# Narrow projections in feature rows with transposes, and unused matmuls at five borders, in a two-block forward pass

## What is computed

```python
# first block
x   = macaron_ffn(x, mod[:, 0:3], *ffn1)          # norm, gate/up (2816), down
ctx = macaron_ffn(ctx, mod_ctx[:, 0:3], *ffn1)
h_ctx_f, h_ctx_b = context_states(ctx, ...)       # h @ w_in[:, x | B | dt]: dt has 2*12 = 24 columns
x, _, _ = mix_sublayer(x, mod[:, 3:6], h_ctx_f, h_ctx_b, *mix)
x = macaron_ffn(x, mod[:, 6:9], *ffn2)
# mix_sublayer: u_f, z, xbc, dt_raw = split(h @ w_in); conv, scan over chunks, fourier part, @ w_out
dt = softplus(dt_raw + dt_bias)                   # (512, 24)
# second block, two layers
h = rmsnorm(x, attn_norm[l]); z = h @ w_in[l]     # q/k/v of four branches A B C D, gates
# vB (64 columns), wI (4, weights of the index heads) and fA (8, forget logits) are narrow; vD has 128
score = einsum('bqhs,bqh->bqs', relu(qI . kI), wI * scale); sel = top_k(score, 128)   # branch B
logf  = log_sigmoid(fA + forget_bias)             # branch A
x = x + sum_n(sigmoid(gate_n) * (y_n @ w_branch_n)) @ w_out[l]
h = rmsnorm(x, ffn_norm[l]); x = x + (silu(a) * b) @ w_down[l]   # a, b from a causal conv of h @ w_up
```

## Time and profile before

| quantity | value |
|---|---|
| median of 3 runs | 3680.62 us (3677.23 to 3682.32) |
| the profiled execution's own time | 3679.27 us |
| its span (first to last instruction) | 3677.9 us |
| mean granted clock of PE | 0.972 of full speed |
| busy: PE, PEld, DVE, ACT, POOL | 3492.6, 2784.7, 1684.8, 1434.5, 1426.5 us |

### The profile page before, as it was taken

The page is one execution under the profiler, slowest core; times in us unless marked ns, Lnnn a source line. Parts: engine busy times, 40 slices in busy tenths (PEclk is TensorE's granted clock), DMA queues, the critical chain, the costliest instruction groups (busy, mean ns, idle before and its releaser), DMA issues.

```text
span 3677.9 us, 45245 instructions
## 1 busy us (share of the span) xinstructions
PE 3492.6 (95%) x17424; PEld 2784.7 (76%) x17424; DVE 1684.8 (46%) x2997; ACT 1434.5 (39%) x2448; POOL 1426.5 (39%) x651
## 2 busy tenths in 40 slices
PE   6899999998899998999999999999999999999998
PEld 4788889786578886876776778887876766778886
DVE  7976464547420115846453243133755453234143
ACT  3223354554532323344443344343344453334342
POOL 3454434321244444334332344444333333344443
PEclk9999999999999998999999999999999999999999
DMA  7574345131123322222222222323222222223232
GB/s 301 193 255 145 124 156 176 64 96 54 46 80 92 103 92 82 87 68 83 75 74 86 88 81 91 100 90 111 83 73 75 73 76 93 80 75 101 95 96 82
DMA packets 118423, 376.45 MB, mean 102 GB/s; under 512 B 15424, under 2 KB 16320, under 8 KB 117952
## 3 DMA queue, kind: packets, MB, share of 16 engines
q1 hardware_dynamic: 107280, 356.33, 29.4%
q10 hardware_dynamic: 10928, 17.22, 1.6%
HBM read 359.86 MB, written 2.10 MB: 98 GB/s over the span
## 4 chain that ended last, share of the span: by engine, by line
PE 76%; DVE 11%; ACT 5%; issue 3%; POOL 2%; DMA 2%; ACTq 1%; SPq 0%; DVEq 0%; POOLq 0%
PE ps L1336 23%; PE ps L1338 22%; PE ps L1337 22%; DVE b L2197 2%; ACT b L1663 2%; POOL b L2561 1%; PE ps L1579 1%; PE ps L1600 1%; ACTq L1769 1%; PE ps L1561 1%; DVE b L2463 1%; PE ps L1623 1%; PE ps L1557 1%; PE ps L1634 1%; DMA b<-in_w 1%
## 5 line engine op out<-in xcount | busy, mean ns | idle before, releaser
L2561 POOL TENSOR_TENSOR b<-b,b 128x1024 fp32r<-128x1024 f32 (+2 forms) x579 | 1326.1, 2290 | 2141.2 <-ACT b L1663 2124.3
L1336 PE MATMUL ps<-b,b 128*128 128x512 f32 (+3 forms) x4848 | 1839.6, 379 | 76.9 <-POOL b L2561 27.5
L1338 PE MATMUL ps<-b,b 128*128 128x512 f32 (+3 forms) x4848 | 1800.4, 371 | 0.0
L1337 PE MATMUL ps<-b,b 128*128 128x512 f32 (+3 forms) x4848 | 1800.3, 371 | 0.0
L1336 PEld LDWEIGHTS ps<-b,b 128*128 128x128 f32 x4848 | 932.0, 192 | 312.3 <-issue 113.3
L1338 PEld LDWEIGHTS ps<-b,b 128*128 128x128 f32 x4848 | 931.3, 192 | 159.5
L1337 PEld LDWEIGHTS ps<-b,b 128*128 128x128 f32 x4848 | 932.6, 192 | 154.6 <-issue 5.0
L1663 ACT ACTIVATE b<-b 128x1024 fp32r<-128x1024 f32 (+2 forms) x622 | 607.2, 978 | 388.9 <-PE ps L1338 254.5
L2112 DVE SCALAR_TENSOR_TENSOR b<-ps,b,b 128x511 f32<-128x511 f32 x88 | 66.0, 750 | 366.7 <-ACT b L1714 366.7
L2197 DVE CUSTOM_DVE_ANT_0 b<-b,b,b 128x1024 bf16<-128x1024 f32 x112 | 216.8, 1936 | 18.0 <-DMA b<-in_ada 6.2
L1724 ACT ACTIVATE b<-b 128x512 fp32r<-128x512 f32 (+1 forms) x110 | 64.9, 590 | 397.2 <-DVE b L2121 294.5
(11 more groups left out here) (231 smaller groups left out, 2371.9 us busy)
## 6 DMA issues: line engine op xcount, KB each, us to landing
b<-in_w SPq DMA_DIRECT2D x458, 512.0 KB, 3.5
b<-in_ada SPq DMA_DIRECT2D x88, 512.0 KB, 5.0
b<-in_w SPq DMA_DIRECT2D x80, 384.0 KB, 3.1
b<-in_w SPq DMA_DIRECT2D x80, 320.0 KB, 2.9
b<-b ACTq DMA_DIRECT2D x176, 64.0 KB, 2.0
b<-in_const SPq DMA_DIRECT2D x24, 256.0 KB, 4.0
b<-in_x SPq DMA_DIRECT2D x1, 2048.0 KB, 16.6
out<-b SPq DMA_DIRECT2D x8, 256.0 KB, 2.5
```

The lines of the kernel that those rows point to most:

```text
L1336: pe.matmul(out, a[0], b[0], start=first, stop=False)
L1337: pe.matmul(out, a[0], b[1], start=False, stop=False)
L1338: return pe.matmul(out, a[1], b[0], start=False, stop=last)
L2561: then(pool.tensor_tensor(wlo[j % NS][:, 0:nk * w], raw[j % NR][:, 0:nk * w], whi[j % NS][:, 0:nk * w].bitcast(F32), ALU.subtract), "lop", j)
```

## The change

The narrow projections `dt`, `cdt`, `vb` and `vd` are now made by `fm` with M = 24, 76 or 128 stationary columns and all tokens streaming (24 matmuls each in place of 96, or of 48 for `cdt`). ACT copies the M x tokens tile out of PSUM (event `nt`), and a step `back`, put behind the next tile's matmuls, transposes it on PE in blocks of 128 tokens (4 or 2 transposes) and copies it to where its readers expect it: on DVE with the bias for `dt` and `cdt`, on ACT for `vb` and `vd`. The readers `wi` and `fg1` come later in the list (behind six gaps, in the thread of `qa`), `fg2` behind the first eight steps of the selection, and the context's softplus (`sp`, s="c") behind `row` and a gap. At the five borders `idle` steps issue matmuls on the high half of the next weight piece, whose results nobody reads: 8 ahead of a `nfin` whose squares DVE adds up, 12 behind each `nfin`, and 3 behind each square of norms 7 and 9. That makes 56 at the first and at the second border and 20 at each other one, 172 in all.

```diff
+    def narrow(self, name, key, ver, N, M, **kw):
+        t = self.fm(name, 0, key, ver, N, M=M, **kw)
+        self.settle()
+        self.step("evac", t=t)
+        self.late.append(dict(kind="back", t=t))
...
+def prenorm(p, c=None):
     nid = PN[p]["norm"]
-    return [do("nfin", nid=nid)] + [do("pn", p=p, i=i) for i in range(8)] + [do("pnlow", p=p)]
+    return (idle(c, 0 if nid in PLAIN else 8) + [do("nfin", nid=nid)] + idle(c, 12)
+            + [do("pn", p=p, i=i) for i in range(8)] + [do("pnlow", p=p)])
+
+def addnorm(a, c=None):
+    return (idle(c, 8) + [do("nfin", nid=AN[a]["norm"])] + idle(c, 12) + [do("an", a=a, i=i) for i in range(8)])
+
+def squares(nid, c=None):
+    return [x for i in range(8) for x in [do("nadd", nid=nid, i=i)] + idle(c, 3)]
...
-    F.tm("dt", 1, "dt", ("pn", 2), 4)
+    F.narrow("dt", "dt", ("pn", 2), L, 24)
+    late, F.late = F.late, []
     S += weave(F)
     F = fore()
+    F.late = late
...
-    F.tm("cdt", 1, "cdt", ("pn", 3), 2)
+    F.narrow("cdt", "cdt", ("pn", 3), LC, 24)
...
-    S += weave(F, [do("sp", s="c"), do("row")] + [do("grp", g=g) for g in range(4)]
+    S += weave(F, [do("row"), do("gap"), do("sp", s="c")] + [do("grp", g=g) for g in range(4)]
...
-    S += weave(F) + addnorm(2) + squares(7) + prenorm(4)
-    S += weave(ffn(2, "ffn2", ("pn", 4), L, 8)) + addnorm(3) + squares(9) + prenorm(5)
+    c = at[0]
+    S += weave(F) + addnorm(2, c) + squares(7, c) + prenorm(4, c)
+    F = ffn(2, "ffn2", ("pn", 4), L, 8)
+    c = at[0]
+    S += weave(F) + addnorm(3, c) + squares(9, c) + prenorm(5, c)
...
-        F.tm("vb", 1, "vbwf", H, 4, l=l)
-        S += weave(F) + [do("wi", l=l)]
+        F.narrow("vb", "vbwf", H, L, 76, l=l)
...
-        F.tm("vd", 1, "vd", H, 4, l=l)
-        S += weave(F, [do("fg1", l=l)] + [do("gap")] * 8 + [do("fg2", l=l)] + select(1) + select(2) + select(3), 1.0)
+        F.narrow("vd", "vd", H, L, 128, l=l)
+        late, F.late = F.late, []
+        B = select(1) + select(2) + select(3)
+        S += weave(F, [do("gap")] * 6 + [do("wi", l=l), do("fg1", l=l), do("gap")] + B[:8] + [do("fg2", l=l)] + B[8:], 1.0)
...
-        S += weave(F) + prenorm(6 + 2 * l)
+        S += weave(F) + prenorm(6 + 2 * l, at[0])
         S += weave(ffn(3 + l, "ffnb", ("pn", 6 + 2 * l), L, 11 + 2 * l, conv=l))
         if l == 0:
-            S += prenorm(7)
+            S += prenorm(7, at[0])
...
                 if k == "mm":
-                    q = 128 * st["q"]
-                    p = three(b[:, 0:N], (wh[:, q:q + 128], wl[:, q:q + 128]), (hi[:, x, 0:N], lo[:, x, 0:N]),
+                    rows = t.get("M", 128)
+                    q = rows * st["q"]
+                    p = three(b[0:rows, 0:N], (wh[:, q:q + rows], wl[:, q:q + rows]), (hi[:, x, 0:N], lo[:, x, 0:N]),
                               st["first"], st["last"])
...
+            elif k == "idle":
+                w = whi[st["c"] % NS]
+                at.wait_ge(*n("hi", st["c"]))
+                b = bank_of(st["bank"])
+                for _ in range(st["n"]):
+                    pe.matmul(b[:, :], w[:, 0:128], w[:, 0:512], start=True, stop=True)
+            elif k == "back":
+                t = st["t"]
+                name, l, rows = t["name"], t.get("l"), t["M"]
+                at.wait_ge(*n("nt", name, l))
+                b = bank_of(st["bank"])
+                for i in range(t["N"] // 128):
+                    p = pe.transpose(b[:, rows * i:rows * i + rows], narrow_at(name)[0:rows, 128 * i:128 * i + 128],
+                                     ident[0:rows, 0:rows])
+                p.then_inc(up("bk", name, l), 1)
```

More of the change, by code:

```diff
@@ L969, with back_event @@
 ROPES = ("qi", "ki", "kd", "qb", "qd", "kc", "qc")
+NARROW = ("dt", "cdt", "vb", "vd")
+def back_event(name, l):
+    return (name,) if l is None else ("vt", name, l)
 def soft(mark, key):
@@ L1230, in program, with narrow_at @@
                11: ("pnq", 7, 7), 12: ("pnq", 8, 7)}
+    def narrow_at(name):
+        return Q[4] if name in ("dt", "cdt") else Q[2]
     def soft_of(key):
```

85 lines of the change are left out of this document (57 added, 28 removed), and 4 rows, old and new, of the table SIGNALS.

## The result

| | before | changed |
|---|---|---|
| median of 4 runs | 3681.04 us (3677.23 to 3682.32) | 3653.86 us (3652.54 to 3656.92) |
| ratio | | 0.9929, 95% interval 0.9912 to 0.9946 |
| span of the profiled execution | 3677.9 us | 3653.1 us |
| mean granted clock of PE | 0.972 | 0.985 |

The account below looks back on a forecast made before the run. PE was taken to bound the kernel, busy 95% of the span. The terms summed to 47.4 us, less 2 for unplaced waits: 45.4, from 3680.6 to 3635 us, range 3622 to 3654.

Parts of the forecast that it names:

- Rival A: From 660 to 1030 us PE only waits longer for DVE and ACT, so `dt` and `cdt` gain nothing: 3651 us, 14%.
- Rival B: The clock falls in the new narrow tiles as in the old, 10.3 us per 24- or 76-column tile: 3655 us, 10%.
- Narrow tiles at the wide pace, clock full in them: A narrow tile becomes 24 wide matmuls of 0.2336 us, 5.6 us however few its output columns, at window clock 1.00.
- Rival F: Matmul cost goes by columns streamed; the narrow tiles' remaining time is a wait that stays: slower, 3691 us, under 1%.
- So DVE is late by 0.4 us, and PE has other pairs of the heads in hand: First heads, layer 0: DVE ends near 1539.4, its first head row is wanted at 1539.0; no loss counted.
- The term of +9.3: Both `vd` tiles: 10.7 us each falls to 5.6 + 0.45, saving 4.6 each, counted in full.
- `cdt`, 5.0: `cdt` tile: 7.1 us falls to 2.9 plus 0.22 of transposes, cold rest gives up to 1.3; ends 2 and 5.3.
- `dt`, 10.9: `dt` tile: 15.6 − 5.6 − 0.45 = 9.6 us saved, with the cold matmuls behind it 10.9; lower end 9.
- `vb` of layer 0, 7.5: Saving cut short because `qa` waits for its weight piece's low half from POOL: 7.5 us, ends 5 and 11.
- `vb` of layer 1, 10.9: Tile saves 8.6 us, the cold clock behind it 2.3; the fourth border gives back a 1 us wait; ends 8 and 12.
- Rival D: Fillers run at half clock at the first two borders, squares end some 12 us late at each: 3657 us, 4%.
- Rival E: From 660 to 1030 us PE waits more for DVE and is granted less clock, 0.81: slower, 3685 us, 2%.

Follow-up runs that it names:

- e1: The changed kernel without its 172 unused matmuls, all narrow tiles still feature by feature: 3653.14 us, ratio 0.9923.
- e3: The changed kernel with `vd` made token by token as before, its copies by ACT: 3650.07 us, ratio 0.9914.
- e5: The changed kernel with 12 selection rounds in place of 16 for the last 128 tokens, so work is left out: 3643.88 us, ratio 0.9899.
- e10: The changed kernel with the selection's last six rounds and mask put among the first heads of group A, nothing left out: 3644.06 us, ratio 0.9893.
- e4: The changed kernel with `dt` and `cdt` token by token and the context's softplus ahead of `row`, as before: 3664.18 us, ratio 0.9955.
- e9: The changed kernel with `cdt` and `vd` token by token and the context's softplus ahead of `row`, as before: 3647.95 us, ratio 0.9908.

## Why the prediction was wrong

The range held 3653.9 by a hair, and the ratio of 0.9929 (3654.5 us of the 3680.6) puts it just outside; the size of the gain was wrong by 18 us. That it comes so near the range at all is luck: the range was widened for rivals A and B, and the most was lost at the first heads, which neither names. The prediction's own last sign came true: all five tiles take 5.6 us, the time is above 3650, and the gain is lost in a queue that I took as covered. By its own steps:

- **Narrow tiles at the wide pace, clock full in them: right.** 5.54, 5.48 and 5.65 us of matmuls against 5.6, and the clock at 1.00. Rival B (the fall stays) is out, by e1 without help of the fillers. Rival F is out: 15.6 us for `dt` were the price of its matmuls, since the same product takes 5.54. The Trainium skill, page "TensorE: Matmul & The Clock Gate", section "LDWEIGHTS (loading the stationary operand)", gives a weight load of P columns as P / 1.2 ns; for 128 that is 107 ns, an estimate from the page. The 0.11 us from one 24-column matmul to the next agree with that, and not with its section "Step-by-step: what each phase is for", by which the number of columns alone would count.
- **"So DVE is late by 0.4 us, and PE has other pairs of the heads in hand": this step failed, and cost most.** DVE ended at 1537.7 and was 3.9 us late, not 0.4. Two things in the step were wrong. I set PE's whole lead of 12.1 us (`vb` and `vd`) against a DVE that starts 8.3 us sooner once. But the selection moves with PE: in e3 PE is 16.7 us sooner at the heads and DVE still idles 3.49 us for it. What counts is what PE wins between the start of the selection and the heads, 5.3 us by `vd`, against a slack of 3.4 us, the idle row; and DVE lost 2.0 us more, because its rotation of `kd` now runs beside POOL's low half, which I had at nothing. Nor did it help that PE has other pairs in hand, since the wait goes through ACT: an exponential at the head of its queue keeps a copy behind it that PE needs for a bank. PE then waits 3.13 us and runs 6.8 us at one half of the clock. The term of +9.3 measured -3.8 (e3, by the medians), 13 us off; e5 and e10 give back 10 of them by taking rounds of the selection from ahead of the heads.
- **`cdt`, 5.0: this step failed too; `dt`, 10.9, came.** By 768.4 15.8 us were won, 10.3 are left at the end (e4), and e9 against e3 puts `cdt` at nothing. So `dt` brought about its 10.9, and all of `cdt` went into waits: PE idles 5 to 6 us more from 755.9 to 1046.4 in the kernels with the new `cdt`, and not more in e9, with the new `dt` alone. Rival A was right for `cdt` and wrong for `dt`. I had named the `cx` stage and set a lower end of 2 for it, but the term itself went in at 5.0, and I had not followed the softplus, which the change puts further back in the list.
- **`vb` of layer 0, 7.5: right in the sum (7.9), wrong in the place.** The wait stood one piece ahead, 2.25 us. In e1 it stands at `qa`, 2.95 us, as forecast.
- **`vb` of layer 1, 10.9: right,** 11.1 with the fourth border, a wait of 0.95 where I had 1.
- **Borders.** The delay of 1.2 us at the second is there (1.4), and the third gains 1.5 of the 1.8, held by the low half as said; by the forecast's own rows (2178.4 against a piece ready at 2176.8) the term should have been 1.6. The fifth gains its 1.5 with or without fillers. The fillers together bring between -0.7 and 5.8 us in four pairs, 2.9 in the mean. Rival D (12 us late) is out: at the full clock a square takes 1.55 us.
- **Rival E (less clock in the long stretch) did not happen:** 0.95 against 0.93.

With what the runs gave for the two failed terms the sum is 45.4 - (15.9 - 10.3) - (9.3 + 3.8) = 26.7 us, against 27.2 measured. The sum closes better than the runs can tell, since e3 and e4 are known to some 5 us each, and the other terms were read from one trace and not taken out one at a time.

## What to carry to other kernels

When two engines run side by side and a change lets one of them off, add up what it wins from the place where the other's chain starts to the next place where they meet, and hold that against the other's chain; the idle row at the meeting point is the slack, and a lead beyond it is lost. What was won ahead of that start moves both and doesn't count. Then look at the queue of the third engine: a step that waits there holds back everything behind it, and a wait of three microseconds on PE can cost as much again in clock. Where that happens, work that nobody needs yet can move behind the meeting point: e10 is 6.0 us under e3 by the medians (0.9893 against 0.9914, with intervals that touch), so there the new `vd` pays.

A stage that gives back what a change won looks, in a sum of local gains, like no change at all. The table of one recurring instruction's starts in both traces shows it at once.
